# Output projection of tiles 1 to 3: from two halves over 512 head dimensions to one pass over all 1,024, in slabs of 256 columns

## The chip, the cores and the metric

One core of a Trainium2 chip runs the program. The metric is device microseconds (us) from start to end, the median of several runs. TensorE (PE) multiplies, VectorE (DVE), ScalarE (ACT) and GpSimd (POOL) work on tiles, SyncE (SP) issues plain transfers, and POOL also issues the indirect ones (gathers).

## The reference, cut to what matters

```
x: 512 tokens x 1024, float32
h   = x + W_out [ FoX(8 heads x 64) || DiffAttn(4 heads x 128) ]( W_in RMSNorm(x) )
      W_out is 1024 x 1024; rows 0-511 belong to FoX, rows 512-1023 to the differential heads
hn  = RMSNorm(h)
PEER, per token and per head (8 heads):
      scores of hn W_q against 2 x 128 sub-keys, top 16 of 16 x 16 sums -> 16 experts, gates g
      h += sum over 8 x 16 experts of  gelu(u_e . hn) * g * v_e      (u, v rows of 1024 floats)
out = RMSNorm(h)
```

## The kernel before

The 512 tokens are four tiles of 128. They are worked in two groups: tile 0 alone (group 0), then tiles 1, 2, 3 together (group 1). Tile 0 passes through attention, output projection and the query and key products first. Then its PEER part begins, on DVE, POOL and the DMA engines: for each of 8 heads and each of 16 experts POOL gathers one row of `u` and one of `v` per token (512 KB each, rings of 4 buffers), DVE makes the dot product with `hn` (L1471, `dot`) and adds the weighted `v` row to `h` (L1507, `add_row`). In one quarter of a head (4 experts) DVE has nine gaps, 0 to 8: dots stand in the even gaps 0, 2, 4, 6 and row additions in the odd gaps 1, 3, 5, 7. This is called the **hosted stage**, because all projections, attention and output projections of tiles 1 to 3 are hosted in these gaps: the pieces of that work, in their order, are spread over the 8 x 4 x 9 gaps in proportion to a cost per piece that is written by hand (`share`), and the list of a gap is `AFTER[...]`. A position is written below as head.quarter.gap, so 5.3.7 is head 5, quarter 3, gap 7. PE, ACT and DVE each take the pieces in that same order. PE and ACT may run ahead of DVE as far as banks and semaphores let them. DVE does its part of a piece (for `outproj`, adding the PSUM bank to `h`) after the dot or row addition of the gap.

In the search quarters DVE also makes the top 16 of the next head: `topk_first` (L1396 to L1408) in gap 8 of quarter 0, and `topk_second` spread over the gaps of quarter 1. ACT computes `gelu` of four hidden values at once, ahead of the pieces of gap 6 (L1132), and it cannot do so before the dot of gap 6.

After the hosted stage comes the **row stage**: the 3 x 8 heads of tiles 1 to 3, where POOL gathers `u` and `v` rows together (1 MB per expert number) and PE adds them up through a diagonal of coefficients (L940).

The pieces of the change:

- `mix` (DVE) normalises the four differential heads of a tile; `mixT` half 1 (PE L711, then ACT L1049) transposes them into `qT`; half 0 does so for FoX.
- `outproj` (PE L811, DVE L1328): group 1 has three tiles and four weight slabs of 1 MB. A slab holds 512 rows x 512 columns of W_out. Slabs 0 and 1 take the FoX half of the dimensions (contraction over 4 chunks of 128), slabs 2 and 3 the differential half, so each 512 columns of `h` are added to twice. Each piece is one bank of 128 x 512.
- Three PSUM banks (`mm0`, `mm1`, `acc0`) serve all these products in turn: a product waits until the bank's user three places ahead of it has been emptied.
- Weight slabs of group 1 go through a ring of two buffers in `w_ring`. The load of a slab waits until the last product with the slab two before it is done (L594).
- The last tile's `mixT` half 1 stands on every engine just ahead of that tile's first product that needs it. What stands behind it on PE waits as well.

Of the kernel before, what the change touches and what calls it, by code (L numbers as in the profile page):

```python
# [64 lines left out]
def weight_slabs(w_in, w_out, peer_w_q, heads):  # L65

    def rows(a):
        return a.reshape(-1, P, a.shape[1]).transpose(1, 0, 2).reshape(P, -1)

    starts = [base + c for base in (0, FOX, 2 * FOX, 3 * FOX + heads, 4 * FOX + heads, 5 * FOX + heads)  # L70
              for c in range(0, FOX, HALF_BANK)]
    d = w_out.shape[0]
    return ([rows(w_in[:, c:c + HALF_BANK]) for c in starts]
            + [rows(w_out[r:r + BANK, c:c + BANK]) for r in range(0, d, BANK) for c in range(0, d, BANK)]
            + [rows(peer_w_q[:, c:c + HALF_BANK]) for c in range(0, peer_w_q.shape[1], HALF_BANK)]
            + [rows(w_in[:, 3 * FOX:3 * FOX + heads])])


def build(nc, x, x_cols, gain_cols, first_halves, slabs, f_cols, b_f, lambda_q1, lambda_k1, lambda_q2, lambda_k2, subln_g,
# [104 lines left out]
    def woven(a, b):  # L184

        def placed(ps):
            total, at, out = sum(share(p) for p in ps), 0.0, []
            for p in ps:
                at += share(p)
                out.append((at / total, p))  # L190
            return out

        return [p for _, p in sorted(placed(a) + placed(b), key=lambda x: x[0])]

    def pieces_of(g):
# [23 lines left out]
        for s in range(steps_of(g, 1)):  # L219
# [1 line left out]
            dif += [("mix", g, t) for t in tiles if s == over(t, 1)]  # L221
            dif += [("mixT", g, last, 0)] if s == 2 else []
            dif += [("mixT", g, t, 1) for t in tiles[:-1] if s == over(t, 1) + 3]
        first_out = [("outproj", g, s, t) for s in range(N_OUT // 2) for t in tiles]
        if g == 0:
            ps += woven(fox, keyed) + [("turn", g, VALUE_SLABS[0] - 1), ("lamrow",)]
            ps += woven(dif, [("project", g, s, 0) for s in VALUE_SLABS] + first_out)
        else:
            ps += woven(fox, projections(g, N_IN // 2, N_IN))
            ps += woven(dif, first_out)  # L230
        for s in range(N_OUT // 2, N_OUT):
            for t in tiles:
                if s == N_OUT // 2 and t == last:
                    ps += [("mixT", g, t, 1)]
                ps += [("outproj", g, s, t)]
                if g == 0 and s == N_OUT // 2:
                    ps += [("factors", g)]
                if s == N_OUT - 1 and t == tiles[0]:
                    ps += [("norm2", g, t)]
# [92 lines left out]
    with ExitStack() as ctx:  # L332
# [196 lines left out]
        def emptied(name):  # L529

            scalar = name[0] in ON_SCALAR
            count = sum((u[0] in ON_SCALAR) == scalar for u in MM[:mm_no[name] + 1])
            return (mm_copied if scalar else mm_drained), count
# [12 lines left out]
        def slab_view(n, sl):  # L546

            w = slab_mem[slab_place(n)[0]]
            if N_IN <= sl < N_IN + N_OUT:
                return w.rearrange("p (c n) -> p c n", n=BANK)  # L550
            return w.rearrange("p (c n) -> p c n", c=KC)

# [32 lines left out]
        def _(sp):  # L585
            sp.dma_start(gain_c[:, :], gain_cols).then_inc(g1_in, 16)
            sp.dma_start(xs[:, :], x_cols[0]).then_inc(xt_in, 16)
            def load_slab(n):

                g, sl = slab_order[n]  # L590
                place, before = slab_place(n)
                if before >= 0:
                    sp.wait_ge(mm_full, slab_last_use[slab_order[before]] + 1)
                sp.dma_start(slab_mem[place], slabs[sl]).then_inc(slab_in[place], 16)  # L594

            mid = KC * SLAB // 2
# [103 lines left out]
        def _(pe):  # L700
            def mm_bank(name):

                n = mm_no[name]
                if n >= len(mm):
                    pe.wait_ge(*emptied(MM[n - len(mm)]))
                return bank_of(n)
# [54 lines left out]
            def piece(kind, *p):  # L761
# [42 lines left out]
                elif kind == "outproj":  # L804
                    g, sl, t = p
                    w = slab(g, N_IN + sl)
                    hf = sl * 2 // N_OUT
                    pe.wait_ge(*emptied(("mixT", t, hf)))
                    bk, j = mm_bank((kind, *p)), GROUPS[g].index(t)
                    for c in range(KC // 2):  # L810
                        last = nc.tensor.matmul(bk[:, :], qT[:, KC // 2 * hf + c, j * P:(j + 1) * P], w[:, c, :],  # L811
                                                start=(c == 0), stop=(c == KC // 2 - 1))
                    last.then_inc(mm_full, 1)
                elif kind == "hT":
                    for hf in range(2):
                        pe.wait_ge(*emptied(("outproj", p[0], N_OUT - 2 + hf, p[1])))
                        transposes(("hT", p[1], hf), lambda j: h[:, p[1], (4 * hf + j) * P:(4 * hf + j + 1) * P])
                        if p[0] == 0 and hf == 0:
                            pe.wait_ge(factors_ready, later)
                            nc.tensor.matmul(mm_bank(("factors",))[:, 0:later * P], ones_block, factor_diag,  # L820
                                             start=True, stop=True).then_inc(mm_full, 1)
# [383 lines left out]
        def _(dve):  # L1205
# [32 lines left out]
            def piece(kind, *p):  # L1238
# [83 lines left out]
                elif kind == "outproj":  # L1322
                    g, sl, t = p
                    bk = mm_wait((kind, *p))
                    if sl >= N_OUT // 2:
                        dve.wait_ge(*emptied(("outproj", g, sl - N_OUT // 2, t)))
                    hs = h[:, t, sl % 2 * BANK:(sl % 2 + 1) * BANK]
# [373 lines left out]
```

## Time and profile before

| | us |
|---|---|
| median of 3 runs (1563.15 to 1564.92) | 1563.33 |
| the profiled execution, its own time | 1566.13 |
| its span, first to last instruction | 1564.3 |
| DVE busy in the span | 1137.6 (73%) |
| PE busy in the span | 1261.1 (81%) |
| POOL busy in the span | 774.2 (49%) |

The busy shares are averages over stages with different limits. The stages have to be read apart: start-up and tile 0's attention (0 to about 190), hosted stage (about 100 to 580, with the densest DVE work from about 190), row stage (580 to the end). A DVE row whose start is earlier than start plus duration of the row before it is normal: successive instructions overlap a little, so the step from start to start is what an instruction costs the engine.

### The profile page before, as it was taken

The numbers are of one execution on the slowest core, as the hardware profiler recorded it, in microseconds if no ns is written. First come the engines' busy times: TensorE is split into PE (matmuls) and PEld (weight loads), VectorE is DVE, ScalarE is ACT, GpSimd is POOL, SyncE is SP. The second block draws the span as 40 slices with busy tenths as digits, with TensorE's granted clock in tenths as the row PEclk, the third lists the DMA queues.
The fourth block names the chain that finished last, engine by engine and source line by source line (L and its number), as shares of the span: only waits on it lengthen the run. The fifth ranks groups of instructions, "written<-read, shape, count | busy, mean of one in ns | idle before, by whom it ended". The sixth has DMA issues, their size and how long they took to land.

```text
span 1564.3 us, 12930 instructions
## 1 busy us (share of the span) xinstructions
PE 1261.1 (81%) x3663; PEld 657.9 (42%) x3663; DVE 1137.6 (73%) x2676; ACT 434.8 (28%) x1069; POOL 774.2 (49%) x650
## 2 busy tenths in 40 slices
PE   9988987897775928989987778777777878778687
PEld 8766654465452613444432323333333333333233
DVE  3357799999999888666666676666666676666664
ACT  3331233343342213222221222222221222222222
POOL 0026576776566773354554445454444444554431
PEclk9999988998788968999999989999899988998989
DMA  9479898998889999999999999999999999999994
GB/s 385 167 278 387 343 345 323 371 367 315 282 280 353 380 377 402 422 422 421 421 421 421 422 422 421 421 422 421 422 421 421 421 422 422 421 422 421 420 422 203
DMA packets 102045, 596.50 MB, mean 381 GB/s; under 512 B 11736, under 2 KB 11736, under 8 KB 46680
## 3 DMA queue, kind: packets, MB, share of 16 engines
q0 software_dynamic: 92160, 536.91, 85.2%
q1 hardware_dynamic: 9816, 58.77, 9.6%
q8 instruction: 31, 0.51, 0.1%
q14 instruction: 38, 0.31, 0.0%
HBM read 593.54 MB, written 2.10 MB: 381 GB/s over the span
## 4 chain that ended last, share of the span: by engine, by line
DMA 36%; PE 15%; DVE 9%; POOL 2%; issue 2%; ACT 2%; DVEq 0%
PE acc L940 13%; DMA map_mem<-in_peer_uv_dram,eidx 9%; DMA v_ring<-in_peer_uv_dram,eidx 6%; DMA v_all<-in_peer_uv_dram,eidx 5%; DMA w_ring<-in_peer_uv_dram,eidx 5%; DMA mix_mem<-in_peer_uv_dram,eidx 5%; DMA u_ring<-in_peer_uv_dram,eidx 4%; DMA act_mem<-in_peer_uv_dram,eidx 2%; PE mm L737 1%; DVE map_mem L1479 1%; ACT diag L1139 1%; DVE w_ring L1479 1%; DVE v_all L1479 1%; DVE v_ring L1479 1%; PE sc L737 1%
## 5 line engine op out<-in xcount | busy, mean ns | idle before, releaser
L653 POOL DMA_INDIRECT u_ring<-in_peer_u_dram,eidx x128 | 162.2, 1267 | 177.0 <-DVE gneg L1456 100.9
L1132 ACT ACTIVATE gel<-hid 128x4 f32<-128x4 f32 x126 | 25.8, 205 | 774.4 <-DVE hid L1479 684.3
L660 POOL DMA_INDIRECT v_ring<-in_peer_v_dram,eidx x128 | 154.3, 1205 | 76.1 <-DVE h L1507 44.1
L1507 DVE SCALAR_TENSOR_TENSOR h<-v_ring,coef,h 128x1024 f32<-128x1024 f32 x128 | 164.4, 1285 | 9.0 <-issue 3.9
L940 PE MATMUL acc<-v_all,diag 128*128 128x512 f32 x240 | 119.1, 643 | 62.8 <-ACT diag L1139 62.8
L1471 DVE CUSTOM_DVE_ANT_0 u_ring<-u_ring,hn 128x1024 f32<-128x1024 f32 x128 | 156.4, 1222 | 11.9 <-DMA u_ring<-in_peer_u_dram,eidx 11.4
L940 PE MATMUL acc<-v_ring,diag 128*128 128x512 f32 x240 | 121.7, 654 | 30.3 <-ACT diag L1139 28.8
L940 PE MATMUL acc<-u_ring,diag 128*128 128x512 f32 x240 | 122.6, 659 | 24.5 <-ACT diag L1139 24.5
L940 PE MATMUL acc<-map_mem,diag 128*128 128x512 f32 x240 | 117.6, 636 | 29.6 <-ACT diag L1139 29.6
L1139 ACT ACTIVATE diag<-ident,coef 128x128 f32<-128x128 f32 x376 | 121.5, 390 | 32.2 <-DVE coef L1497 21.6
L737 PE MATMUL mm<-act_mem,w_ring 128*128 128x384 f32 x336 | 114.6, 497 | 8.4 <-ACT act_mem L1057 8.4
L674 POOL DMA_INDIRECT map_mem<-in_peer_uv_dram,eidx x60 | 72.7, 1212 | 87.2 <-PE acc L940 80.9
L674 POOL DMA_INDIRECT u_ring<-in_peer_uv_dram,eidx x60 | 69.6, 1160 | 89.0 <-PE acc L940 81.9
L674 POOL DMA_INDIRECT v_all<-in_peer_uv_dram,eidx x60 | 71.2, 1186 | 81.6 <-PE acc L940 74.6
L674 POOL DMA_INDIRECT v_ring<-in_peer_uv_dram,eidx x60 | 69.3, 1155 | 79.2 <-PE acc L940 72.7
L1479 DVE CUSTOM_DVE_ANT_0 map_mem<-map_mem,hn 128x1024 f32<-128x1024 f32 x60 | 72.9, 1226 | 48.2 <-DMA map_mem<-in_peer_uv_dram,eidx 48.2
L940 PEld LDWEIGHTS acc<-v_all,diag 128*128 128x128 f32 x240 | 48.2, 206 | 128.0 <-issue 95.2
L1479 DVE CUSTOM_DVE_ANT_0 v_all<-v_all,hn 128x1024 f32<-128x1024 f32 x60 | 72.9, 1225 | 38.6 <-DMA v_all<-in_peer_uv_dram,eidx 38.5
L940 PE MATMUL acc<-w_ring,diag 128*128 128x512 f32 x168 | 83.0, 640 | 21.2 <-ACT diag L1139 21.1
L940 PE MATMUL acc<-act_mem,diag 128*128 128x512 f32 x168 | 82.6, 638 | 20.6 <-ACT diag L1139 20.6
L1479 DVE CUSTOM_DVE_ANT_0 v_ring<-v_ring,hn 128x1024 f32<-128x1024 f32 x58 | 70.4, 1226 | 38.3 <-DMA v_ring<-in_peer_uv_dram,eidx 38.3
L1479 DVE CUSTOM_DVE_ANT_0 u_ring<-u_ring,hn 128x1024 f32<-128x1024 f32 x58 | 70.4, 1225 | 38.0 <-DMA u_ring<-in_peer_uv_dram,eidx 38.0
(271 smaller groups left out, 2341.0 us busy)
## 6 DMA issues: line engine op xcount, KB each, us to landing
w_ring<-in_slabs_dram SPq DMA_DIRECT2D x37, 1024.0 KB
v_ring<-in_slabs_dram SPq DMA_DIRECT2D x6, 1024.0 KB, 10.6
u_ring<-in_slabs_dram SPq DMA_DIRECT2D x4, 1024.0 KB, 11.9
h<-in_x_dram SPq DMA_DIRECT2D x4, 512.0 KB, 12.5
u_ring<-in_peer_u_dram,eidx POOLq DMA_INDIRECT x128
v_ring<-in_peer_v_dram,eidx POOLq DMA_INDIRECT x128
v_all<-in_x_cols_dram SPq DMA_DIRECT2D x3, 512.0 KB, 6.5
out_dram<-fin SPq DMA_DIRECT2D x3, 512.0 KB, 7.9
```

What stands on the lines that cost most here:

```text
L653: nc.gpsimd.indirect_dma_start(out=u_ring[:, c % U_RING, :], out_offset=None, in_=peer_u[0], in_offset=bass.IndirectOffsetOnAxis(ap=eidx[n ...
L660: nc.gpsimd.indirect_dma_start(out=v_ring[:, c % V_RING, :], out_offset=None, in_=peer_v[0], in_offset=bass.IndirectOffsetOnAxis(ap=eidx[n ...
L674: nc.gpsimd.indirect_dma_start(out=row_mem[place], out_offset=None, in_=peer_uv, in_offset=bass.IndirectOffsetOnAxis(ap=eidx[n % 3][:, c:c ...
L737: last = nc.tensor.matmul(bk[:, 0:n], w[:, c, q * P:(q + 1) * P], actT[:, c, 0:n], start=(c == 0), stop=(c == KC - 1))
L940: last = nc.tensor.matmul(acc[half][:, :], diag[:, c % COLS, :], v_row(n, c)[:, half * BANK:(half + 1) * BANK], start=first, stop=(n % PH ...
L1132: nc.scalar.activation(gel[:, par, g0:g0 + COLS], hid[:, par, g0:g0 + COLS], ACT.Gelu).then_inc(gelu_done, 1)
L1139: nc.scalar.activation(diag[:, c, :], ident[:, :], ACT.Copy, scale=coef[:, par, g0 + c:g0 + c + 1]).then_inc(diag_done, 1)
L1471: nc.vector.tensor_tensor_reduce(out=u_ring[:, c % U_RING, :], in0=u_ring[:, c % U_RING, :], in1=hn[:, :], scale=1.0, scalar=0.0, op0=ALU. ...
L1479: nc.vector.tensor_tensor_reduce(out=u_row(n, c), in0=u_row(n, c), in1=hn[:, :], scale=1.0, scalar=0.0, op0=ALU.mult, op1=ALU.add, accum_o ...
L1507: nc.vector.scalar_tensor_tensor(out=ht, in0=v_ring[:, c % V_RING, :], scalar=coef[:, par, c:c + 1], in1=ht, op0=ALU.mult, op1=ALU.add).th ...
```

## The change

For group 1 a slab now holds all 1,024 rows of W_out and 256 columns. `outproj` for tiles 1 to 3 contracts over 8 chunks of 128 and gives 128 x 256, which is added to `h` once. There are still four slabs of 1 MB and twelve pieces. Group 1's first two slabs are no longer woven into the differential heads; all twelve pieces stand behind them. The last tile's `mixT` stands ahead of its piece of slab 0. Group 0 keeps its form.

```diff
@@ -73,6 +73,7 @@
     return ([rows(w_in[:, c:c + HALF_BANK]) for c in starts]
             + [rows(w_out[r:r + BANK, c:c + BANK]) for r in range(0, d, BANK) for c in range(0, d, BANK)]
             + [rows(peer_w_q[:, c:c + HALF_BANK]) for c in range(0, peer_w_q.shape[1], HALF_BANK)]
+            + [rows(w_out[:, c:c + HALF_BANK]) for c in range(0, d, HALF_BANK)]
             + [rows(w_in[:, 3 * FOX:3 * FOX + heads])])
 
 
@@ -221,16 +222,16 @@
             dif += [("mix", g, t) for t in tiles if s == over(t, 1)]
             dif += [("mixT", g, last, 0)] if s == 2 else []
             dif += [("mixT", g, t, 1) for t in tiles[:-1] if s == over(t, 1) + 3]
-        first_out = [("outproj", g, s, t) for s in range(N_OUT // 2) for t in tiles]
+        first_out = [("outproj", g, s, t) for s in range(N_OUT // 2) for t in tiles] if g == 0 else []
         if g == 0:
             ps += woven(fox, keyed) + [("turn", g, VALUE_SLABS[0] - 1), ("lamrow",)]
             ps += woven(dif, [("project", g, s, 0) for s in VALUE_SLABS] + first_out)
         else:
             ps += woven(fox, projections(g, N_IN // 2, N_IN))
-            ps += woven(dif, first_out)
-        for s in range(N_OUT // 2, N_OUT):
+            ps += dif
+        for s in range(len(first_out) // len(tiles), N_OUT):
             for t in tiles:
-                if s == N_OUT // 2 and t == last:
+                if s == len(first_out) // len(tiles) and t == last:
                     ps += [("mixT", g, t, 1)]
                 ps += [("outproj", g, s, t)]
                 if g == 0 and s == N_OUT // 2:
@@ -546,7 +547,7 @@
         def slab_view(n, sl):
 
             w = slab_mem[slab_place(n)[0]]
-            if N_IN <= sl < N_IN + N_OUT:
+            if slab_order[n][0] == 0 and N_IN <= sl < N_IN + N_OUT:
                 return w.rearrange("p (c n) -> p c n", n=BANK)
             return w.rearrange("p (c n) -> p c n", c=KC)
 
@@ -591,6 +592,8 @@
                 place, before = slab_place(n)
                 if before >= 0:
                     sp.wait_ge(mm_full, slab_last_use[slab_order[before]] + 1)
+                if g and N_IN <= sl < N_IN + N_OUT:
+                    sl += N_OUT + 2 * PH * P // SLAB
                 sp.dma_start(slab_mem[place], slabs[sl]).then_inc(slab_in[place], 16)
 
             mid = KC * SLAB // 2
@@ -804,16 +807,22 @@
                 elif kind == "outproj":
                     g, sl, t = p
                     w = slab(g, N_IN + sl)
-                    hf = sl * 2 // N_OUT
+                    hf = 1 if g else sl * 2 // N_OUT
                     pe.wait_ge(*emptied(("mixT", t, hf)))
                     bk, j = mm_bank((kind, *p)), GROUPS[g].index(t)
+                    if g:
+                        for c in range(KC):
+                            last = nc.tensor.matmul(bk[:, 0:SLAB], qT[:, c, j * P:(j + 1) * P], w[:, c, :],
+                                                    start=(c == 0), stop=(c == KC - 1))
+                        last.then_inc(mm_full, 1)
+                        return
                     for c in range(KC // 2):
                         last = nc.tensor.matmul(bk[:, :], qT[:, KC // 2 * hf + c, j * P:(j + 1) * P], w[:, c, :],
                                                 start=(c == 0), stop=(c == KC // 2 - 1))
                     last.then_inc(mm_full, 1)
                 elif kind == "hT":
                     for hf in range(2):
-                        pe.wait_ge(*emptied(("outproj", p[0], N_OUT - 2 + hf, p[1])))
+                        pe.wait_ge(*emptied(("outproj", p[0], N_OUT // 2 * (hf + 1) - 1 if p[0] else N_OUT - 2 + hf, p[1])))
                         transposes(("hT", p[1], hf), lambda j: h[:, p[1], (4 * hf + j) * P:(4 * hf + j + 1) * P])
                         if p[0] == 0 and hf == 0:
                             pe.wait_ge(factors_ready, later)
@@ -1322,6 +1331,10 @@
                 elif kind == "outproj":
                     g, sl, t = p
                     bk = mm_wait((kind, *p))
+                    if g:
+                        hs = h[:, t, sl * SLAB:(sl + 1) * SLAB]
+                        nc.vector.tensor_tensor(out=hs, in0=bk[:, 0:SLAB], in1=hs, op=ALU.add).then_inc(mm_drained, 1)
+                        return
                     if sl >= N_OUT // 2:
                         dve.wait_ge(*emptied(("outproj", g, sl - N_OUT // 2, t)))
                     hs = h[:, t, sl % 2 * BANK:(sl % 2 + 1) * BANK]
```

The planner's costs are untouched, so twelve pieces with the same shares are spread again. Before, the DVE additions stood at 4.2.8, 4.3.7, 5.0.8, 5.2.0, 5.3.1, 6.0.1, 6.0.5, 6.0.7, 6.1.0, 6.1.2, 6.1.6 and 6.1.8. Now they stand at 5.3.3, 5.3.5, 5.3.7, 6.0.0, 6.0.2, 6.0.4, 6.0.6, 6.0.7, 6.1.0, 6.1.2, 6.1.6 and 6.1.8. The steps of the differential heads and the `mix` of tiles 1, 2 and 3 come earlier (tile 3's `mix` at 5.3.1 instead of 6.0.3). Everything up to 4.2.5 and everything from 6.1.0 on keeps its position, except that tile 3's `mixT` goes from 6.1.0 to 5.3.7.

DVE in the kernel before, from the dot of gap 6.0.6 to the addition of tile 3's first product behind its `mixT` (the L1471 rows are one dot, L1507 a row addition, `h<-mm` with 512 columns an output-projection addition):

```order
L1471 ISA u_ring,hid<-u_ring,hn 128x1024
L1471 ISA hid 128x1
L1507 SCALAR_TENSOR_TENSOR h<-v_ring,coef,h 128x1024
L1328 TENSOR_TENSOR h<-mm,h 128x512
L1396 MAX tk_v<-store 128x8 x2
L1399 MATCH_REPLACE tk_w<-tk_v,store 128x128 x2
...
L1422 MAX top_v<-cand 128x8
L1471 ISA u_ring,hid<-u_ring,hn 128x1024
L1471 ISA hid 128x1
L1328 TENSOR_TENSOR h<-mm,h 128x512
```

DVE in the changed kernel, from the dot of gap 5.3.6 on, the same chain (L1484 is the dot, L1520 the row addition, L1336 the output-projection addition):

```order
L1484 ISA u_ring,hid<-u_ring,hn 128x1024
L1484 ISA hid 128x1
L1520 SCALAR_TENSOR_TENSOR h<-v_ring,coef,h 128x1024
L1336 TENSOR_TENSOR h<-mm,h 128x256
L1476 RECIPROCAL gsum<-gsum 128x1
L1478 TENSOR_SCALAR gate<-gexp,gsum 128x16
L1484 ISA u_ring,hid<-u_ring,hn 128x1024
L1484 ISA hid 128x1
L1336 TENSOR_TENSOR h<-mm,h 128x256
```

Between the dot that `gelu` waits for and the addition of tile 3's product there stood a row addition, an addition, the whole of `topk_first` and a dot. Now there stands a row addition alone.

PE in the kernel before, from the last values of the differential heads (L922) to the end of the output projection (`ident,mix_mem` is a `mixT`, 4 rows of L811 are listed for one product of 512 columns):

```order
L922 MATMUL o<-v_all,map_mem 128x128 x4
L811 MATMUL acc<-w_ring,store 128x512 x4
L811 MATMUL mm<-w_ring,store 128x512 x8
L711 MATMUL acc<-ident,mix_mem 128x128 x4
L811 MATMUL mm<-w_ring,store 128x512 x8
L811 MATMUL acc<-w_ring,store 128x512 x4
L811 MATMUL mm<-w_ring,store 128x512 x4
```

PE in the changed kernel, the same place (8 rows of L815 are one product of 256 columns):

```order
L931 MATMUL o<-v_all,map_mem 128x128 x4
L815 MATMUL mm<-w_ring,store 128x256 x16
L714 MATMUL acc<-ident,mix_mem 128x128 x4
L815 MATMUL mm<-w_ring,store 128x256 x16
L815 MATMUL acc<-w_ring,store 128x256 x8
L815 MATMUL mm<-w_ring,store 128x256 x16
L815 MATMUL acc<-w_ring,store 128x256 x8
L815 MATMUL mm<-w_ring,store 128x256 x16
L815 MATMUL acc<-w_ring,store 128x256 x8
L815 MATMUL mm<-w_ring,store 128x256 x8
```

Behind the last `mixT` there stood four products and now stand ten; ahead of it, behind the last values, three and now two.

## Rows read from the trace of the kernel before

**Rows 1.** Busy time by engine in the hosted and the row stage, with clock and DMA

```profile
core 0: us, PE busy (x) PEld busy (x) DVE busy (x) ACT busy (x) POOL busy (x), PEclk, DMA share, GB/s
190.00:580.00 390.00, 296.71 (x1187) 190.06 (x1186) 367.73 (x759) 143.27 (x297) 269.44 (x217) 0.86 0.91 333
580.00:1560.00 980.00, 788.78 (x1716) 339.19 (x1716) 672.37 (x1675) 233.26 (x613) 449.63 (x380) 0.92 1.00 413
```

**Rows 2.** POOL in order of time: last gather of tile 0, first of row stage

```profile
571.49 0.94 POOL L660 DMA_INDIRECT v_ring<-in_peer_v_dram,eidx  x1 [0.77 <-DVE h L1507]
572.73 1.21 POOL L674 DMA_INDIRECT v_all<-in_peer_uv_dram,eidx  x1 [0.30 <-issue]
```

**Rows 3.** DVE by instruction: additions of 512 columns, one sum of 256 columns

```profile
L1328 DVE TENSOR_TENSOR h<-mm,h x12: 683/690/704, 75.2 to 496.3; 128x512 f32<-128x512 f32 x12
L1408 DVE TENSOR_TENSOR cand<-tk_v x32: 406/417/426, 98.0 to 1477.5; 128x256 f32<-128x256 f32 x32
```

**Rows 4.** DVE in order of time, 474 to 483: dot of 6.0.6 to addition at 6.1.0

```profile
474.31 1.22 DVE L1471 CUSTOM_DVE_ANT_0 u_ring<-u_ring,hn 128x1024 f32<-128x1024 f32 x1
475.45 1.28 DVE L1507 SCALAR_TENSOR_TENSOR h<-v_ring,coef,h 128x1024 f32<-128x1024 f32 x1
476.65 0.69 DVE L1328 TENSOR_TENSOR h<-mm,h 128x512 f32<-128x512 f32 x1
477.25 0.48 DVE L1396 MAX8 tk_v<-store 128x8 f32<-128x128 f32 x2
...
480.38 1.21 DVE L1471 CUSTOM_DVE_ANT_0 u_ring<-u_ring,hn 128x1024 f32<-128x1024 f32 x1
...
482.44 0.69 DVE L1328 TENSOR_TENSOR h<-mm,h 128x512 f32<-128x512 f32 x1 [0.84 <-PE mm L811]
```

**Rows 5.** ACT in order of time, the same place

```profile
475.57 0.20 ACT L1132 ACTIVATE gel<-hid 128x4 f32<-128x4 f32 x1 [3.75 <-DVE hid L1471]
475.68 0.67 ACT L1049 ACTIVATE store<-acc,sub_c 128x512 f32<-128x512 f32 x1
```

**Rows 6.** PE in order of time, 471 to 493: last `mixT`, last four products

```profile
471.51 0.66 PE L711 MATMUL acc<-ident,mix_mem 128*128 128x128 f32 x4 [1.01 <-DVE mix_mem L1320]
476.45 9.38 PE L811 MATMUL mm<-w_ring,store 128*128 128x512 f32 x16 [4.29 <-ACT store L1049]
485.67 3.60 PE L811 MATMUL acc<-w_ring,store 128*128 128x512 f32 x8
489.11 3.60 PE L811 MATMUL mm<-w_ring,store 128*128 128x512 f32 x8
```

**Rows 7.** Stretches of 10 us, same columns as rows 1

```profile
470.00:480.00 10.00, 4.70 (x11) 1.93 (x10) 9.60 (x28) 2.36 (x4) 6.25 (x6) 0.71 1.00 399
480.00:490.00 10.00, 10.00 (x24) 4.46 (x23) 9.03 (x21) 0.00 (x0) 4.83 (x3) 0.95 0.84 305
```

**Rows 8.** Products of 256 columns over 8 chunks: PE in order of time, weight loads

```profile
187.03 7.07 PE L729 MATMUL mm<-w_ring,act_mem 128*128 128x256 f32 x32
193.94 3.62 PE L729 MATMUL acc<-w_ring,act_mem 128*128 128x256 f32 x16
...
L729 PEld LDWEIGHTS acc<-w_ring,act_mem x80: 186/190/192, 183.5 to 359.6; 128*128 128x128 f32 x80
```

**Rows 9.** DVE in order of time: gates (L1463, L1465), next dot; coefficients, next row addition

```profile
461.82 0.15 DVE L1463 RECIPROCAL gsum<-gsum 128x1 f32<-128x1 f32 x1
...
462.27 1.23 DVE L1471 CUSTOM_DVE_ANT_0 u_ring<-u_ring,hn 128x1024 f32<-128x1024 f32 x1
...
463.42 0.16 DVE L1497 TENSOR_TENSOR coef<-gel,gate 128x4 f32<-128x4 f32 x1
463.67 1.28 DVE L1507 SCALAR_TENSOR_TENSOR h<-v_ring,coef,h 128x1024 f32<-128x1024 f32 x1
```

**Rows 10.** Weight slabs: one load's issue; ns and landing over all loads

```profile
463.66 0.33 SPq L594 DMA_DIRECT2D w_ring<-in_slabs_dram  x1
...
DMA to landing us min/median/max: 4.7/10.6/14.5
```

## The prediction

> **What bounds the kernel now.** I read the stages first, by busy time in long windows. In the hosted stage, 190 to 580, DVE is busy 367.73 of 390 us and the DMA engines 0.91; in the row stage the DMA engines are at 1.00 and DVE at 672 of 980 [rows 1]. So two limits follow each other: DVE until tile 0's rows are done, then the transfers of 1 MB rows. The hand-over shows how they are joined. POOL's last gather for tile 0 waits for a DVE row addition, and the first gather of the row stage is issued right behind it [rows 2]. The row stage has a fixed number of bytes at a full DMA, so a microsecond that DVE loses or gains in the hosted stage moves the start of the row stage, and the end, by about a microsecond. I take that ratio as 1; a smaller one is a rival below.
>
> Then I read where DVE waits in the output projection. In order of time it waits once, 0.84 us, for PE's product L811, at tile 3's first product behind its `mixT` [rows 4]. All other additions of tiles 1 to 3 find their bank filled. The chain behind that wait is readable on three engines. The dot of gap 6.0.6 is over at 475.45 (start of the next DVE row, [rows 4]). `gelu` starts at 475.57, and only behind it does ACT copy the transposed `mix` of tile 3, at 475.68 [rows 5]. PE starts the product at 476.45, after 4.29 us of idle time that ACT's copy ended [rows 6], and DVE adds at 482.44. That is 6.99 us from the end of the dot to the addition. DVE hid 6.15 us of it: a row addition of 1.20, an addition of 0.60, `topk_first` and the first step of `topk_second` together 3.13, a dot of 1.14 (steps from start to start [rows 4]; the rest is small change). The PE part of the chain was long because the clock had fallen: a product at full clock takes 3.44 us (485.67 to 489.11), whereas the two from 476.45 to 485.67 took 9.22, so the first took 5.78 [rows 6]. The granted clock was 0.71 in 470 to 480, that is partly the 1.2 GHz level, after PE had stood idle from 472.17 [rows 6, 7].
>
> **The change, part by part.**
>
> *DVE additions.* Twelve of 512 columns become twelve of 256. The median row of 512 is 0.690 us; the nearest row of 256 float32 columns is 0.417 [rows 3]. Saved: 12 x 0.273 = 3.3 us. The 256-column row reads both operands from SBUF, which could be off for a PSUM operand; bounds are nothing saved beyond the fixed part (12 x 0.1, about 1) and half of 0.69 (4.1). I take 3.3, since 0.417 is also what a fixed 0.14 plus half the rest gives.
>
> *PE products.* 4 chunks x 512 columns become 8 chunks x 256: the same columns streamed, twice as many instructions. Rows of just this shape exist for the value projections: two products in 7.07 us and the next 6.91 after (187.03 to 193.94), so 3.46 each [rows 8]. Against 3.44 for 512 columns this costs nothing. It speaks against the change that each product has eight more weight loads, of 190 ns [rows 8]; if they lay open, a product would be 1.5 us longer. The rows say that they are hidden. The Trainium skill (TensorE: Matmul & The Clock Gate, section LDWEIGHTS) makes a load last as long as its 128 columns take, whatever is streamed behind it, about 107 ns; by that alone, if nothing overlapped, the twelve products would gain 8 x 0.107 = 0.9 us each. The trace disagrees on the length (190 ns) and shows the overlap.
>
> *Slab loads.* Same four loads of 1 MB. The third slab's load now goes out when tile 3's product with the first is done, and its first use is three products later, 10.3 us. Landing takes 4.7 to 14.5 us, median 10.6 [rows 10]. Before, the fourth slab went out at 463.66 [rows 10] and was in use at about 482. I price this at nothing, with up to 4.2 us (14.5 - 10.3) at the top of the range.
>
> *The order.* This is the large term. The differential heads lose the woven products, but DVE did not wait for PE there (the only wait of any size is ACT's square root, which stays), so nothing is gained. Behind them, tile 3's `mixT` stands at 5.3.7, directly after the `gelu` of gap 6, with only a row addition of DVE work between the dot and the addition that needs the product. And behind `mixT` PE now has ten products in line instead of four, six of them due on DVE one or two gaps apart. PE cannot use its time before: it stands at the transposes while DVE makes three dots, two row additions and two short additions, 3 x 1.14 + 2 x 1.20 + 2 x 0.33 = 6.5 us, longer than the idle time before the same place now. So I take the low clock again, and the same 6.99 us chain.
>
> Now the walk, with 0 at the end of the dot of 5.3.6, a short addition at 0.60 - 0.27 = 0.33, gates 0.45 and coefficients 0.25 [rows 9]. PE ends its first product at 6.78 and then one every 3.44; DVE sees each 0.21 later (482.23 to 482.44 [rows 4, 6]).
> - 5.3.7: DVE free at 1.20, product at 6.99: waits 5.79.
> - 6.0.0: 6.99 + 0.33 + 0.45 + 1.14 = 8.91, product at 10.43: waits 1.52.
> - 6.0.2: 10.43 + 0.33 + 0.25 + 1.20 + 1.14 = 13.35, at 13.87: waits 0.52.
> - 6.0.4 and 6.0.6: each 2.67 of work against 3.44: wait 0.77 and 0.77.
> - 6.0.7: 20.75 + 0.33 + 1.20 = 22.28, at 24.19: waits 1.91.
> - 6.1.0: `topk_first` stands between: 24.19 + 0.33 + 3.13 + 1.14 = 28.79, product at 27.63: no wait, and none after.
>
> The waits sum to 11.3 us. The 0.84 of before goes, and 3.3 are saved by shorter additions: 11.3 - 0.8 - 3.3 = +7.2 us. What is queued behind the waiting DVE addition are dots and row additions; POOL waits for these to free the rings, and so the row stage comes later by as much. Against the profiled execution that makes a span of 1571.5 and its own time 1573.3 (1566.13 + 7.2); its own time lay 2.8 above the median, so the median becomes 1563.3 + 7.2 = 1570.5.
>
> **The rivals.**
> - *The clock stays up.* PE has been busy with the first two products shortly before. Then the first product takes 3.44 and everything shifts by 2.34: waits 9.0, sum +4.9, 1568.2. Against it stands the idle time of 6.5 us. Chance 15%. In the other direction, two products wholly at 1.2 GHz would cost 6.88 each, 4.5 more than taken: 1575.0; chance 5%.
> - *The third slab is late.* Up to 4.2 us more at 6.0.6: up to 1574.7. For it: the median landing is about the time that there is. Against it: DVE's waits starve the gathers, so the load has the DMA engines to itself. Chance 5%.
> - *Open weight loads.* Six products each 1.5 us longer: +9, 1579.6. The section named above would allow it; the rows of this shape do not. Chance 1%.
> - *The waits are absorbed.* If the last part of the hosted stage is already bound by transfers (4 buffers in each ring, DMA 0.91 on the mean), DVE's delay is made up by 580, and so is its saving: within 3 us, about 1563 to 1566. For it: the high DMA share. Against it: in 480 to 490 the DMA share is only 0.84 while DVE is busy 9.03 of 10 [rows 7], so the queue has run dry there before too, and no backlog is carried over that could be worked off. Chance 16%.
> - *Faster: the other sign.* PE reaches tile 3's product in time, and only the shorter additions count: -3.3 - 0.8, 1559.2. It needs the whole chain from the end of the dot within the 1.20 us row addition, or waits of under 4.1 us in total. `gelu`, copy and one product alone are 1.00 + 3.44. It decides otherwise only if ACT's copy went out before `gelu`, which the order does not allow. Chance 8%.
>
> **How the numbers follow.** My forecast holds 50%. A difference below 0.2%, 3.1 us, can hardly be told from no change for this kernel. Slower by more than that: forecast 50, clock up 15, longer low clock 5, late slab 5, loads 1, together 76%. Same: 16%. Faster: 8%. The range leaves out the faster case and the far ends of the dearest: 1562.5 to 1575.0. The likeliest is 1570.5, its own range 1568 to 1573.
>
> **What the profile after would show.** The DVE waits for PE's product: one of 5 to 6 us at the third addition, four or five of 0.5 to 2 us behind it, none from 6.1.0 on. PE idle for over 5 us before tile 3's first product, its clock low there, ten products then without a gap. Additions of about 0.42 us. DMA share down in the same 25 us, and the first gather of the row stage some 7 us later. I am wrong if that gather moves and the end does not, if PE's products behind `mixT` take over 3.5 us each, or if DVE's waits in the differential heads, now none, turn out to have been hidden in the rows.

## The result, and the profile of the changed kernel

| | before | changed |
|---|---|---|
| median of 5 runs, us | 1564.41 (1563.15 to 1564.92) | 1572.39 (1569.01 to 1572.81) |
| ratio, with 95% interval | | 1.0045 (1.003 to 1.006) |
| profiled execution, its own time | 1566.13 | 1569.95 |
| its span | 1564.3 | 1568.2 |

The changed kernel is slower: the ratio of 1.0045 is 7.0 us on 1564.41 (its interval 4.7 to 9.4), and 7.2 were forecast. The two medians themselves lie 8.0 us apart. In a later session the kernel gave the same ratio again (e7).

DVE in order of time in the changed kernel, the row addition of gap 5.3.7 and the output-projection additions behind it; what stands in brackets is DVE's wait and what ended it. These rows answer to [rows 4].

```profile
458.67 0.42 DVE L1336 TENSOR_TENSOR h<-mm,h 128x256 f32<-128x256 f32 x1
...
460.15 1.28 DVE L1520 SCALAR_TENSOR_TENSOR h<-v_ring,coef,h 128x1024 f32<-128x1024 f32 x1
466.86 0.42 DVE L1336 TENSOR_TENSOR h<-mm,h 128x256 f32<-128x256 f32 x1 [5.43 <-PE mm L815]
...
470.31 0.42 DVE L1336 TENSOR_TENSOR h<-mm,h 128x256 f32<-128x256 f32 x1 [1.42 <-PE mm L815]
...
473.77 0.42 DVE L1336 TENSOR_TENSOR h<-acc,h 128x256 f32<-128x256 f32 x1 [0.44 <-PE acc L815]
...
477.22 0.42 DVE L1336 TENSOR_TENSOR h<-mm,h 128x256 f32<-128x256 f32 x1 [0.69 <-PE mm L815]
...
480.67 0.42 DVE L1336 TENSOR_TENSOR h<-mm,h 128x256 f32<-128x256 f32 x1 [0.69 <-PE mm L815]
...
484.13 0.42 DVE L1336 TENSOR_TENSOR h<-acc,h 128x256 f32<-128x256 f32 x1 [1.84 <-PE acc L815]
...
488.73 0.42 DVE L1336 TENSOR_TENSOR h<-mm,h 128x256 f32<-128x256 f32 x1
```

Six waits, 10.51 us in sum, where the kernel before had one of 0.84; none for the first two additions and none from 6.1.0 (488.73) on. From 466.86 to 484.13 the steps between the additions are 3.45 us each: DVE moves at PE's pace.

The same place on ACT and on PE, in order of time. They answer to [rows 5] and [rows 6].

```profile
460.26 0.20 ACT L1141 ACTIVATE gel<-hid 128x4 f32<-128x4 f32 x1 [6.16 <-DVE hid L1484]
460.38 0.67 ACT L1058 ACTIVATE store<-acc,sub_c 128x512 f32<-128x512 f32 x1
```

```profile
453.80 0.66 PE L714 MATMUL acc<-ident,mix_mem 128*128 128x128 f32 x4 [0.87 <-DVE mix_mem L1329]
461.14 9.13 PE L815 MATMUL mm<-w_ring,store 128*128 128x256 f32 x32 [6.69 <-ACT store L1058]
470.11 3.62 PE L815 MATMUL acc<-w_ring,store 128*128 128x256 f32 x16
473.57 7.07 PE L815 MATMUL mm<-w_ring,store 128*128 128x256 f32 x32
480.47 3.62 PE L815 MATMUL acc<-w_ring,store 128*128 128x256 f32 x16
```

The dot ends at 460.15, `gelu` runs at 460.26, the copy at 460.38, the product from 461.14, the addition at 466.86: the chain of the kernel before, 6.71 us long. PE had stood idle for 6.69. Its first two products took 8.97 (461.14 to 470.11), the first therefore 5.5, every other one 3.45.

Stretches of time in the changed kernel, same columns as [rows 1].

```profile
584.00:1564.00 980.00, 788.18 (x1716) 338.88 (x1716) 672.35 (x1676) 232.79 (x613) 450.64 (x379) 0.93 0.99 413
...
460.00:470.00 10.00, 8.86 (x32) 7.51 (x33) 3.39 (x8) 0.78 (x2) 3.75 (x4) 0.74 0.90 319
470.00:480.00 10.00, 10.00 (x48) 8.81 (x47) 8.44 (x13) 0.00 (x0) 6.43 (x6) 1.00 0.75 242
```

DVE is busy 3.39 of 10 us while it waits, PE's clock is 0.74 there and then full, and the row stage is what it was, at 413 GB/s. The additions by instruction, and POOL's first gather of the row stage:

```profile
L1336 DVE TENSOR_TENSOR h<-mm,h x9: 416/422/425, 456.0 to 501.8; 128x256 f32<-128x256 f32 x9
```

```profile
575.19 0.94 POOL L663 DMA_INDIRECT v_ring<-in_peer_v_dram,eidx  x1 [0.79 <-DVE h L1520]
576.44 1.22 POOL L677 DMA_INDIRECT v_all<-in_peer_uv_dram,eidx  x1 [0.30 <-issue]
```

An addition takes 0.422 us. The gather comes 3.7 us later than before [rows 2], and the span is 3.9 longer. This profiled execution is one of the quicker ones of the changed kernel (1569.95 against a median of 1572.39), and the one of the kernel before is slower than its median (1566.13 against 1564.41).

### The profile page after: what moved, and what is told of

The parts are those of the page before. It is cut to its first block, busy times and chain, and to the rows that moved or that the text cites. A ratio compares the mean times of both kernels' runs of the same rounds, so it can differ in the third digit from the quotient of the medians.

```text
span 1568.2 us, 13113 instructions
## 1 busy us (share of the span) xinstructions
PE 1263.3 (81%) x3759; PEld 679.0 (43%) x3759; DVE 1135.3 (72%) x2676; ACT 430.8 (27%) x1066; POOL 774.3 (49%) x650
## 4 chain that ended last, share of the span: by engine, by line
DMA 34%; PE 15%; DVE 11%; POOL 2%; ACT 2%; issue 1%; DVEq 0%
PE acc L949 13%; DMA u_ring<-in_peer_uv_dram,eidx 7%; DMA v_ring<-in_peer_uv_dram,eidx 6%; DMA map_mem<-in_peer_uv_dram,eidx 5%; DMA act_mem<-in_peer_uv_dram,eidx 5%; DMA mix_mem<-in_peer_uv_dram,eidx 4%; DMA w_ring<-in_peer_uv_dram,eidx 3%; DMA v_all<-in_peer_uv_dram,eidx 3%; PE mm L740 2%; DVE v_ring L1492 1%; DVE u_ring L1492 1%; ACT diag L1148 1%; DVE map_mem L1492 1%; DVE v_all L1492 1%; PE sc L740 1%
## 5 line engine op out<-in xcount | busy, mean ns | idle before, releaser
L949 PE MATMUL acc<-v_all,diag 128*128 128x512 f32 x240 | 128.5, 685 | 70.0 <-ACT diag L1148 70.0
L1520 DVE SCALAR_TENSOR_TENSOR h<-v_ring,coef,h 128x1024 f32<-128x1024 f32 x128 | 164.5, 1285 | 8.0 <-DMA v_ring<-in_peer_v_dram,eidx 3.9
L1484 DVE CUSTOM_DVE_ANT_0 u_ring<-u_ring,hn 128x1024 f32<-128x1024 f32 x128 | 156.3, 1221 | 12.4 <-DMA u_ring<-in_peer_u_dram,eidx 12.1
L949 PE MATMUL acc<-u_ring,diag 128*128 128x512 f32 x240 | 117.0, 633 | 28.0 <-ACT diag L1148 28.0
L949 PE MATMUL acc<-v_ring,diag 128*128 128x512 f32 x240 | 116.9, 633 | 27.2 <-ACT diag L1148 27.2
L677 POOL DMA_INDIRECT v_all<-in_peer_uv_dram,eidx x60 | 75.5, 1258 | 100.4 <-PE acc L949 93.8
L949 PEld LDWEIGHTS acc<-v_all,diag 128*128 128x128 f32 x240 | 51.9, 223 | 140.8 <-issue 107.5
L949 PE MATMUL acc<-w_ring,diag 128*128 128x512 f32 x168 | 79.6, 618 | 14.0 <-ACT diag L1148 14.0
## 6 DMA issues: line engine op xcount, KB each, us to landing
v_ring<-in_slabs_dram SPq DMA_DIRECT2D x6, 1024.0 KB, 10.8
```

Of the source, the lines that this page charges most:

```text
L677: nc.gpsimd.indirect_dma_start(out=row_mem[place], out_offset=None, in_=peer_uv, in_offset=bass.IndirectOffsetOnAxis(ap=eidx[n % 3][:, c:c ...
L949: last = nc.tensor.matmul(acc[half][:, :], diag[:, c % COLS, :], v_row(n, c)[:, half * BANK:(half + 1) * BANK], start=first, stop=(n % PH ...
L1484: nc.vector.tensor_tensor_reduce(out=u_ring[:, c % U_RING, :], in0=u_ring[:, c % U_RING, :], in1=hn[:, :], scale=1.0, scalar=0.0, op0=ALU. ...
L1520: nc.vector.scalar_tensor_tensor(out=ht, in0=v_ring[:, c % V_RING, :], scalar=coef[:, par, c:c + 1], in1=ht, op0=ALU.mult, op1=ALU.add).th ...
```

## The experiments

Times from here on are from later sessions, in which single runs of the kernel before spread from 1559 to 1570 us. Each comparison is with the kernel before in the same session. Because differences of 2 to 3 us are near the noise, the verdict on a mechanism rests on DVE's waits first, and then on when the first gather of the row stage is issued. One profile places that gather only to about 3 us: the two profiles of the changed kernel have it at 576.44 and 579.28. From that gather to the end of the span it is 989.4 to 993.4 us in all eleven profiles, so what arrives there late ends late.

**e1: ACT's copy ahead of gelu**

```diff
+    EARLY_COPY = ("mixT", 1, GROUPS[1][-1], 1)
...
                             if gap == 2 * COLS - 2:
+                                if EARLY_COPY in pieces_in(n, grp, gap + 1):
+                                    piece(*EARLY_COPY)
                                 gelu(n, n % 2, grp * COLS)
                             for p_ in pieces_in(n, grp, gap):
-                                piece(*p_)
+                                if p_ != EARLY_COPY:
+                                    piece(*p_)
```

> The changed kernel, with one difference: ACT copies tile 3's transposed mix ahead of the gelu of gap 5.3.6 instead of behind it. Theory (the chain dot, gelu, copy, product, with PE idle and its clock low before it, makes the first wait, and the others follow from ten products in line): the first DVE wait, 5.43 us in the changed kernel, goes to nothing, and the waits behind it stay at 0.2 to 1.9 us, 4.2 in sum instead of 10.5. Time 6.3 lower than the changed kernel, about 1564.5 to 1566, no longer separable from the kernel before. Rival (PE's products in half-width form or the slab loads are what costs): the copy matters little, the waits stay at 9 or more in sum, the time stays above 1569.

Measured: 1567.60 against 1565.55, ratio 1.0013 (1.0000 to 1.0026). DVE and PE in order of time:

```profile
466.46 0.42 DVE L1340 TENSOR_TENSOR h<-mm,h 128x256 f32<-128x256 f32 x1 [1.78 <-PE mm L816]
469.92 0.42 DVE L1340 TENSOR_TENSOR h<-mm,h 128x256 f32<-128x256 f32 x1 [1.42 <-PE mm L816]
```

```profile
457.05 0.66 PE L715 MATMUL acc<-ident,mix_mem 128*128 128x128 f32 x4 [2.03 <-DVE mix_mem L1333]
459.82 10.05 PE L816 MATMUL mm<-w_ring,store 128*128 128x256 f32 x32 [2.11 <-DVE h L1340]
469.71 3.62 PE L816 MATMUL acc<-w_ring,store 128*128 128x256 f32 x16
```

The first wait fell from 5.43 to 1.78, the sum from 10.5 to 6.85; 4.2 were expected. The product now starts as soon as DVE empties its bank (459.82), not behind ACT's copy. But the clock fell all the same: two products took 9.89 (459.82 to 469.71) instead of 6.9, and those 3 us account for the miss: 1.78 at the first wait, and 1.42 instead of 0.2 at the second. The time missed its forecast too (1564.5 to 1566); it is still 2.1 above the kernel before. The chain through `gelu` is confirmed by the waits. The rest of the waits, PE's pace, stays.

**e2: the new order with the old products**

```diff
-            ps += woven(dif, first_out)
-        for s in range(N_OUT // 2, N_OUT):
+            ps += dif
+        for s in range(0 if g else N_OUT // 2, N_OUT):
```

> The kernel before (512 columns, two halves, added twice) with only the order changed: no product woven into the differential heads, all twelve behind them. The first two slabs' products need only the FoX half, so they do not wait for tile 3's mixT, which stays at 6.1.0. Theory (it is the dependence of the first slab's third product on tile 3's mixT that leaves PE idle, not the crowding alone): DVE waits under 2 us in sum, time 1563.5 to 1565.5, as before. Rival (crowding twelve products behind the heads is enough): DVE waits of 4 us or more, time 1567 or more.

Measured: 1563.27 against 1565.55, ratio 0.9996 (0.9981 to 1.0011). DVE has no wait for a product at all. PE in order of time:

```profile
458.13 7.10 PE L811 MATMUL mm<-w_ring,store 128*128 128x512 f32 x16 [0.43 <-DVE h L1328]
465.07 3.60 PE L811 MATMUL acc<-w_ring,store 128*128 128x512 f32 x8
468.50 7.03 PE L811 MATMUL mm<-w_ring,store 128*128 128x512 f32 x16
475.37 0.60 PE L711 MATMUL acc<-ident,mix_mem 128*128 128x128 f32 x4
```

Twelve products behind the heads cost nothing when the first six need only the FoX half: PE works through, at full clock, up to three banks ahead of DVE. So it is not the unweaving by itself. It is that a product over all dimensions needs tile 3's `mixT`, which stands early in a line of twelve.

**e3: what a microsecond of DVE is worth**

```diff
                     nc.vector.tensor_tensor(out=hs, in0=bk[:, :], in1=hs, op=ALU.add).then_inc(mm_drained, 1)
+                    if g:
+                        link(nc.vector.tensor_tensor(out=xs[:, BANK:D], in0=g2b[:, 0:BANK], in1=g2b[:, BANK:D], op=ALU.add))
```

> The kernel before with a dummy DVE addition of 128 x 512 behind each of the twelve additions of tiles 1 to 3, written to memory that is free there; DVE waits for its end, so each costs about 0.73 us, 8.8 in sum. It measures what a microsecond of DVE in the hosted stage is worth at the end. Theory of a ratio of 1: 1573.2. Rival (part is absorbed where the end of the hosted stage is bound by transfers, as the changed kernel's first row-stage gather suggests, 3.7 us later for 6.4 us of net waits): a ratio of about 0.6, 1569.5.

Measured: 1574.44 against 1565.55, ratio 1.0064 (1.0042 to 1.0085), that is 10.0 us with an interval of 6.6 to 13.3 (the medians differ by 8.9). DVE in order of time, a dummy and what follows it, and then POOL's first gather of the row stage:

```profile
468.31 0.68 DVE L1330 TENSOR_TENSOR xs<-g2b 128x512 f32<-128x512 f32 x1
469.03 1.23 DVE L1473 CUSTOM_DVE_ANT_0 u_ring<-u_ring,hn 128x1024 f32<-128x1024 f32 x1
```

```profile
579.08 1.21 POOL L674 DMA_INDIRECT v_all<-in_peer_uv_dram,eidx  x1 [0.30 <-issue]
```

One costs 0.72 (468.31 to 469.03), twelve 8.6; the 0.84 wait goes, which leaves 7.8. The first gather of the row stage comes 6.4 us later (579.08 against 572.73). The interval holds a ratio of 1 and lies above what 0.6 would give (0.6 x 8.6 = 5.2). The gather moved by about 0.8 of the 7.8, but with the scatter of 3 us between two profiles this does not tell 0.8 from 1.

**e4: two other products behind mixT**

```diff
+        if g:
+            in_line[2:6] = [(1, tiles[0]), (1, tiles[1]), (0, last), (1, last)]
+            ps += [("outproj", g, s, t) for s, t in in_line[:2]] + [("mixT", g, last, 1)]
+            in_line = in_line[2:]
...
```

> The changed kernel with another order of products: behind tile 3's mixT stand slab 1 for tiles 1 and 2, then slab 0 and slab 1 for tile 3. PE has two products to do while gelu and the copy are awaited, but slab 0 comes free only two products before slab 2 is needed. Theory: the first wait of 5.4 us goes to about 0.5, and at slab 2's first product (6.0.6) a wait of 3 to 5 us for the weight load comes in its place; waits 7 to 9 in sum, time 1569 to 1571. If loads land in 6 us or less, nearer to 1568.5; if they take the median 10.6 of all loads, no gain against the changed kernel.

Measured: 1571.42 against 1565.55, ratio 1.0033 (1.0015 to 1.0050). DVE, then PE, then SP in order of time:

```profile
482.66 0.42 DVE L1342 TENSOR_TENSOR h<-mm,h 128x256 f32<-128x256 f32 x1 [7.63 <-PE mm L821]
```

```profile
458.18 7.14 PE L821 MATMUL mm<-w_ring,store 128*128 128x256 f32 x32 [2.11 <-DVE h L1342]
...
477.46 5.15 PE L821 MATMUL mm<-w_ring,store 128*128 128x256 f32 x16 [5.24 <-DMA w_ring<-in_slabs_dram]
```

```profile
468.81 0.33 SPq L603 DMA_DIRECT2D w_ring<-in_slabs_dram  x1
```

As foreseen, one wait took the other's place, and it was dearer than foreseen, 7.63 instead of 3 to 5. The load went out at 468.81 and PE could start at 477.46, 8.65 us later, and after 5.24 us without work the product ran at the low clock (5.15 us). The waits sum to 10.8 where 7 to 9 were expected, no better than the changed kernel's. Three of the twelve executions took 1564.1 to 1566.3 us and the other nine 1570.9 to 1574.5; the profiled one (1574.31) is of the nine, and what the three had is not on record.

The 8.65 us are no measure of the changed kernel's margin. There the load goes out when tile 3's first product is done (466.85) and the slab is needed 10.2 us later, at 477.0 (473.57 + 3.45). What the DMA engines did meanwhile differs. The first row below is e4 while it waits for its slab, the second the changed kernel in its profile of e7, where the load went out at 468.56 and the slab was needed at 478.7:

```profile
468.80:477.50 8.70, 3.46 (x17) 2.70 (x16) 5.52 (x8) 0.20 (x1) 6.85 (x6) 0.97 0.97 353
...
474.50:476.50 2.00, 2.00 (x11) 1.77 (x10) 1.56 (x4) 0.00 (x0) 1.69 (x2) 1.00 0.02 8
```

In e4 DVE was busy for 5.52 of the 8.7 us, POOL went on gathering, and the engines moved 353 GB/s. In the changed kernel DVE stood still right before, few gathers were issued, and from 474.50 on the engines had next to nothing to do (0.02, 8 GB/s). So the slab had landed within 5.9 us of its issue, some 4 us before it was needed.

**e5: the additions further apart**

```diff
         if kind == "outproj":
-            return SHARE_ROWS[1]
+            return SHARE_ROWS[1] if p[1] == 0 else 5.0
```

> The changed kernel with one number changed: the planner's share of a group-1 output projection is 5.0 instead of 3.6. The twelve additions then stand at 5.2.6, 5.2.8, 5.3.2, 5.3.5, 5.3.7, 6.0.1, 6.0.3, 6.0.6, 6.0.8, 6.1.2, 6.1.6 and 6.1.8; tile 3's mixT stands at 5.3.2, five gaps of DVE work behind the gelu of 5.2.6. Theory (placement makes the waits, not the form): DVE waits 0 to 4 us in sum instead of 10.5, the first gather of the row stage 7 to 9 us earlier than in the changed kernel, its median 1562 to 1565 and 6 to 9 below the changed kernel in the same session. Rival (the form itself costs, or the heads pressed together make new waits): waits stay above 7 us, somewhere, and the time within 3 us of the changed kernel.

Measured: 1566.23 against 1564.41, ratio 1.0013 (1.0002 to 1.0024); the changed kernel in the same session had 1571.43. DVE in order of time:

```profile
388.99 0.56 DVE L1369 CUSTOM_DVE_ANT_0 map_mem<-sc,act_mem 128x384 f32<-128x384 f32 x1 [0.96 <-PE sc L889]
...
458.07 0.42 DVE L1336 TENSOR_TENSOR h<-mm,h 128x256 f32<-128x256 f32 x1 [0.75 <-PE mm L815]
...
464.98 0.42 DVE L1336 TENSOR_TENSOR h<-acc,h 128x256 f32<-128x256 f32 x1 [0.25 <-PE acc L815]
...
471.88 0.42 DVE L1336 TENSOR_TENSOR h<-mm,h 128x256 f32<-128x256 f32 x1 [0.69 <-PE mm L815]
```

The waits for products fell from 10.5 to 1.7. The waits for PE in the heads grew: 0.86, 1.10 and 0.96 us from 337 on, where the kernel before had one of 0.81. Of the loss, 5.2 of 7.0 us are gone by changing one number of the placement, with the form of the products untouched. Both forecasts of the time were missed by a little: 1562 to 1565, and 6 to 9 below the changed kernel. It does not beat the kernel before, though its profiled execution has its first row-stage gather 1.6 us ahead of it (571.17). That execution (1563.69) is 2.5 us quicker than its median, so it does not stand for the median. One thing in which executions of this order of work differ shows between e5 and e8, whose programs are the same up to 6.3. PE in e5 and then in e8, at tile 3's first product, and the stretch of two products in each, columns as in [rows 1]:

```profile
454.34 7.14 PE L815 MATMUL mm<-w_ring,store 128*128 128x256 f32 x32 [2.48 <-ACT store L1058]
...
454.47 8.83 PE L815 MATMUL mm<-w_ring,store 128*128 128x256 f32 x32 [2.57 <-ACT store L1058]
```

```profile
454.34:461.32 6.98, 6.98 (x32) 6.16 (x33) 6.14 (x11) 1.20 (x1) 5.74 (x5) 1.00 0.95 325
...
454.47:463.14 8.67, 8.67 (x32) 7.33 (x33) 6.13 (x11) 1.20 (x1) 5.56 (x5) 0.80 0.91 319
```

After nearly the same idle time the clock stayed up in e5 (1.00) and fell in e8 (0.80), which cost e8 1.7 us. How often either happens is not shown.

**e6: PE kept busy**

```diff
+                        pe.wait_ge(subk_in, 16)
                     transposes(("mixT", t, hf), ...)
+                    if (g, t, hf) == (1, GROUPS[1][-1], 1):
+                        for _ in range(14):
+                            nc.tensor.matmul(o_b[:, 0:2 * K1], ident[:, :], subkT[:, 0:2, :]..., start=True, stop=True)
```

> The changed kernel with fourteen dummy products of 256 columns behind tile 3's transposes (constants into a PSUM bank that is free by then), about 6.0 us of PE work in the 6.7 us in which PE stood idle. Theory: the granted clock stays at its upper level, tile 3's first product takes 3.4 to 3.5 us instead of 5.6, the first DVE wait 3.1 instead of 5.4, the waits in sum 8.1 instead of 10.5, the time 2.3 lower than the changed kernel. Rival (the clock does not matter, or the dummies delay the product): first wait 5 us or more.

Measured: 1569.98 against 1564.41, ratio 1.0039 (1.0027 to 1.0052). PE and DVE in order of time:

```profile
454.06 6.21 PE L810 MATMUL o<-subkT,ident 128*128 128x256 f32 x28
460.91 7.15 PE L820 MATMUL mm<-w_ring,store 128*128 128x256 f32 x32 [0.65 <-issue]
```

```profile
464.64 0.42 DVE L1341 TENSOR_TENSOR h<-mm,h 128x256 f32<-128x256 f32 x1 [3.45 <-PE mm L820]
```

With dummy work in the gap the two products took 7.0 us instead of 9.0, and the first wait was 3.45 instead of 5.43; the sum is 8.5. So about 2 us of the loss are the clock. The medians (1569.98 against 1571.43 for the changed kernel) agree in sign, but are too close to settle it alone.

**e7: the changed kernel again**

> The changed kernel itself, once more, on the same chip as the two above, as their common measure. Expected: the same six DVE waits, 10 to 11 us in sum, 4 to 10 us slower than the kernel before.

Measured: 1571.43 against 1564.41, ratio 1.0045 (1.0028 to 1.0062). The first wait on DVE, and POOL's first gather of the row stage:

```profile
468.56 0.42 DVE L1336 TENSOR_TENSOR h<-mm,h 128x256 f32<-128x256 f32 x1 [5.88 <-PE mm L815]
```

```profile
579.28 1.22 POOL L677 DMA_INDIRECT v_all<-in_peer_uv_dram,eidx  x1 [0.30 <-issue]
```

The other five waits are the same to 0.01 us (1.42, 0.44, 0.69, 0.69, 1.84); all six sum to 10.96. The gather comes 6.6 us later than before [rows 2], 2.9 later than in the first profile of the same program.

**e8 and e9: the same kind of wait elsewhere**

```diff
                             if gap == 2 * COLS - 2:
                                 gelu(n, n % 2, grp * COLS)
+                                if (n, grp) == (6, 3):
+                                    piece("query", 1, 1)
                             for p_ in pieces_in(n, grp, gap):
-                                piece(*p_)
+                                if p_ != ("query", 1, 1):
+                                    piece(*p_)
```

> The spaced version (planner's share 5.0) with one more change on ACT: in quarter 6.3 gelu stands ahead of the copy of the second query product instead of behind it. In every profile so far DVE waits 2.3 to 3.5 us there for gelu, because ACT waits for PE's product first: the same kind of wait as the one behind tile 3's mixT. Theory: that wait (3.5 us in the spaced version) goes to under 0.5, no other takes its place, the first gather of the row stage comes 4 to 5 us earlier than in the kernel before, and the median is 1560 to 1563, 2 to 4 below the kernel before in the same session. Rival (that part of the hosted stage is bound by transfers already): the wait goes, waits for u and v rows behind it grow by as much, time as the kernel before.

> The kernel before with the same single change on ACT. It parts the gain of the order on ACT from that of the new output projection. Theory: 2 to 3 us below the kernel before. Rival as above: no difference.

Measured: e8 1567.12 against 1564.54, ratio 1.0022 (1.0007 to 1.0038); e9 1563.87, ratio 0.9994 (0.9982 to 1.0005). e8 is thus a little slower than the kernel before, where 2 to 4 us less were expected. The wait for `gelu` in quarter 6.3 is gone in both. In the kernel before it is this row; the profile names no releaser, but ACT's `gelu` runs at 522.37, right ahead of it. In e3 the wait was 1.52, below the 2.3 to 3.5 that the expectation gives for every profile.

```profile
522.61 0.16 DVE L1497 TENSOR_TENSOR coef<-gel,gate 128x4 f32<-128x4 f32 x1 [2.99 <-issue]
```

A little further on, in order of time, e8 and then e9 show:

```profile
529.56 1.23 DVE L1487 CUSTOM_DVE_ANT_0 u_ring<-u_ring,hn 128x1024 f32<-128x1024 f32 x1 [3.40 <-DMA u_ring<-in_peer_u_dram,eidx]
```

```profile
526.71 1.22 DVE L1474 CUSTOM_DVE_ANT_0 u_ring<-u_ring,hn 128x1024 f32<-128x1024 f32 x1 [2.29 <-DMA u_ring<-in_peer_u_dram,eidx]
```

The waits speak for the rival: here, where weight slabs and gathers share the DMA engines (their busy share from 515 to 530 is 1.00 in the kernel before and 0.99 in e8 and e9), DVE runs into a wait for a gathered row that is nearly as long. In e8 the first gather of the row stage comes at 572.32, 0.4 us earlier than before instead of 4 to 5. In e9 it comes at 569.84, 2.9 earlier, but 1.3 of these stood already at tile 3's product (added at 481.15 instead of 482.44), ahead of the edit. The times settle e8, not e9: its interval leaves room for a gain of up to 2.8 us, and 2 to 3 were expected. e8's wait at tile 3's product was also longer than e5's (2.44 instead of 0.75), by the clock shown above. None of these versions beats the kernel before beyond its interval.

## Why the prediction was right, step by step

- **Where the cost would be.** DVE's waits stand at the six additions that were named, and at none other: forecast 5.79, 1.52, 0.52, 0.77, 0.77, 1.91; measured 5.43, 1.42, 0.44, 0.69, 0.69, 1.84. The walk from one addition to the next, with steps taken from rows of the kernel before, was good to 0.1 us a step apart from the first.
- **The chain.** 6.71 us instead of 6.99. e1 took it apart: without `gelu` ahead of the copy, the first wait falls to 1.78, all of it clock.
- **The clock.** It fell as forecast (first product 5.5 instead of 5.78), and e6 shows its price, 2 us. In the second profile (e7) the two products took 9.42, so the price is not fixed.
- **The order.** The prediction put the cost on the dependence on `mixT` with ten products behind it. e2 (same order, old form, no wait) and e5 (same form, other spacing, 1.7 us of waits) bound it from both sides. One reading beside it was off: in the kernel before DVE does wait for PE in the differential heads, once, 0.81 us at 378.93. In the two profiles of the changed kernel that wait is 0.41 and 0.93, so nothing hung on it.
- **Additions.** 0.690 became 0.422, 12 x 0.268 = 3.2 us against 3.3 forecast.
- **Weight loads of PE.** Hidden: 3.45 us a product. With that the rival of open weight loads is out, beside which the prediction names the Trainium skill (TensorE: Matmul & The Clock Gate, section LDWEIGHTS).
- **The slab load.** No wait, and the price of nothing was right for the reason that the prediction gave against its own rival: DVE's waits leave the DMA engines to the load, which landed within 5.9 us in e7. In e4, where the gathers went on, the same kind of load took 8.65.
- **The ratio of 1.** This step is confirmed only roughly. e3 bounds it: 6.6 to 13.3 us for a net 7.8 of DVE time, so 0.6 is out and 1 is in. The gathers scatter about it. Net waits (waits less 0.8 and 3.2) against the delay of the first row-stage gather are 6.5 and 3.7 us in the first profile, 6.9 and 6.6 in the second, 2.8 and 4.6 in e1, 6.8 and 6.4 in e4, 4.5 and 4.3 in e6. In the first profile the other waits on DVE between 495 and the end of the stage also shrank, from 8.8 to 6.8 us (sum of eight and of six bracketed waits, most of them for gathered rows and `gelu`), so part of the delay can be absorbed there; how much of it is scatter is not shown.
- **The sum.** 7.2 us forecast and 7.0 measured agree more closely than the parts deserve, and that is luck. The waits were 0.8 us (0.3 in e7) smaller than forecast, the interval of the ratio runs from 4.7 to 9.4 us, and the medians of the first session differ by 8.0.

## What to carry to other kernels

When a product is made to depend on an input that comes last, look at what is queued behind it on the in-order engine and how far apart the results are due: shorter additions saved 3.2 us, but ten products of 3.45 us, due every 2.7, came to stand behind one late transpose. A copy that stands behind another engine's milestone (here `gelu` behind the fourth dot) needs as much cover between the two as its whole chain is long, clock included. And check with a dummy load what a microsecond of the busy engine is worth before you sum: here 7.8 us of added work cost 6.6 to 13.3 us, while taking away a wait of 3 us at a spot where the gathers were as close to the bound gave nothing that stands clear of the noise.

## What the runs showed of the hardware that was not expected

The granted clock after a short pause was not the same from one execution to the next. In e5 and e8 PE has the same work up to tile 3's first product and stood idle for 2.48 and 2.57 us before it; the two products behind took 6.98 us at a granted clock of 1.00 in e5, and 8.67 at 0.80, that is partly at the 1.2 GHz level, in e8. In e1, after pauses of 2.03 and 2.11 us with four transposes between, the first product ran at 0.54 and the two took 9.89; in e4, after 0.88 and 2.11 us, the two took 6.98. A weight slab of 1 MB was in use 8.65 us after its issue where gathers ran beside it (e4, 353 GB/s in all), and had landed within 5.9 us where DVE's waits had held the gathers back (e7).
